# A two-layer encoder trunk on one core: VectorE's transposes in groups of four between weight splits, also in the first step; norm weights in four pieces; rope angles later; the last gate ahead of the next stage's units

## The chip, the cores and the metric

The kernel runs on one core of a Trainium2 chip. The time is device microseconds (us) of one execution. The kernel before took 1093.1 us (median of 3 runs, 1093.0 to 1094.49). All matrix products run on TensorE (PE in the profile), element-wise work on VectorE (DVE), ScalarE (ACT) and GpSimd (POOL); SyncE (SP) only issues DMAs.

## The reference

Two layers (`l`), each of four sublayers, and each sublayer followed by a LayerNorm of the residual. Sequence 256, width 1024, hidden width 2816. Cut to what matters:

```python
def reference(x, mem, positions, ln_g, ln_b, ...):
    for l in range(DEPTH):
        x = layer_norm(ALPHA * x + 0.5 * swiglu(x, ffn1_w13[l], ffn1_w2[l]), ln_g[l, 0], ln_b[l, 0])
        h = x @ w_in[l]
        ...
        y_pool = pool_mixer(u_pool, pool_w[l], pool_scale[l])
        y_mla = mla_mixer(c_q, c_kv, k_pe, positions, q_norm_g[l], w_uq[l], kv_norm_g[l], w_ukv[l])
        y_mix = jnp.concatenate([y_pool, y_mla], axis=-1) @ w_out[l]
        x = layer_norm(ALPHA * x + y_mix, ln_g[l, 1], ln_b[l, 1])
        x = layer_norm(ALPHA * x + memory_cross_attention(x, mem, ...), ln_g[l, 2], ln_b[l, 2])
        x = layer_norm(ALPHA * x + 0.5 * swiglu(x, ffn2_w13[l], ffn2_w2[l]), ln_g[l, 3], ln_b[l, 3])

def swiglu(x, w13, w2):
    gate, up = jnp.split(x @ w13, 2, axis=-1)
    return (jax.nn.silu(gate) * up) @ w2

def layer_norm(x, g, b):                  # in f32
    y = (x - mean(x)) * rsqrt(var(x) + LN_EPS) * g + b
```

Everything is f32.

## The kernel before

**Products and units.** Each f32 matrix is used as a rounded part (hi) and a remainder (lo), both in the type f32r, and a product is three matmuls: hi·hi, hi·lo, lo·hi. Weights come in 366 units of 128x1024 numbers. SP loads a unit into one of four `raw` slots, ScalarE rounds it (`split_hi`, L1180), VectorE subtracts (`split_lo`, L1429), and TensorE takes it from one of six slots (`w_hi`/`w_lo`, and two cut from `v_flat` and `cqp`). SP waits for `lo_done` of the unit four before: a raw slot comes free when VectorE is through with it.

**Order.** Each engine's program is written out by hand in the same order of stages: `ffn(0,0)`, norm 0, `mix(0)` (projection, pool mixer, attention, `w_out`), norm 1, `memory(0)`, norm 2, `ffn(0,1)`, norm 3, and the same for layer 1. Norms are numbered `e` = 0 to 7. TensorE counts milestones on one semaphore, `pe_done`; a `Plan` numbers them before the program is written, and `done[tag]` is the count at which `tag` is reached. `ahead(tag)` on ScalarE and VectorE splits as many of the coming units as find a free slot by that milestone, `ahead_to(n)` all up to unit n.

**A feed-forward stage** has 11 steps (`FS`). With `u` its first unit, a step `s` is four units of w13 (`up`, PSUM banks of 128x512), ScalarE's silu (`gate`, L1222), VectorE's product (`multiply`, L1472) into `ev`, then the 256 tokens x 256 hidden columns are turned into columns, rounded (`round_hidden`, L1230) and split (`split_hidden`, L1492), and two units of w2 follow (`down`). TensorE runs `up(s+1)` before `down(s)`. For steps 1 to 9 (`by_blocks`) VectorE turns the hidden block itself, with 16 STREAM_TRANSPOSEs (L1486) right behind `multiply`; for step 0 and step 10 TensorE does it with four transposes through the identity (`turn_hidden`, L854). Steps 2 to 9 stand in a hardware loop.

**A residual stage** such as `w_out` has eight row units. `row_tail` runs the last five for token block 0 first (milestone `("y", e, 0)`), then `second_block` does token block 1: first its left half for all five (`("half y", e)`), then its right half, and only in that last pass is a unit's milestone counted:

```python
for c in range(2):
    for i, n in enumerate(units):
        ...
        last = row_block(n, acts[i], 1, False, i == len(units) - 1, [c])
        if c == 1:
            reach(last, ("unit", n), *([("y", e, 1)] if i == len(units) - 1 else []))
    if c == 0:
        reach(last, ("half y", e))
```

**A norm** (VectorE's `norm`, odd part for e = 1 and 5): `residual(0, ·)` (L1535), `mean(0)`, `center(0)` (L1546: subtract the mean, times `ln_g`), `variance(0)` (L1551), `residual(1, 0)`, `shift(0)` (L1559: times the reciprocal deviation that GpSimd made at L1815, plus `ln_b`), then one unit split, `residual(1, 1)` and the same for token block 1. TensorE transposes the normed block (`turn`, L674) as soon as `norm_done` says so, block 0 right behind the row stage and block 1 inside the next filler product. `gb` holds `ln_g` and `ln_b`, each spread over all 128 partitions; GpSimd loads it (`load_gains`, L1808, two DMAs of 512 KB), for norms 1 and 5 after the pool mixer, which uses `gb` as scratch, for norm 0 after the rope tables, whose angles are made in `gb` too, and else when the norm before is finished. `center` waits for all of a norm's DMAs:

```python
dve.wait_ge(gains_landed, 32 * (e + 1))
```

## Time and profile before

| | before |
|---|---|
| median of 3 runs | 1093.1 us (1093.0 to 1094.49) |
| the profiled execution | 1093.56 us |
| its span | 1091.7 us |
| PE busy | 1081.4 us, 5720 matmuls |
| DVE busy | 847.9 us, 1450 instructions |
| ACT busy | 534.4 us, 731 instructions |
| POOL busy | 80.8 us, 120 instructions |
| read from memory | 201.41 MB, 185 GB/s over the span |

Busy is the time in which an engine had an instruction in work; the span is the time from the first to the last instruction. The execution is 1.9 us longer than its span. In the rows further down, a timeline row is start, duration, engine, line, operation, what it writes and reads, its shapes, and how many instructions it merges; in square brackets the idle time before it and what ended it. Matmuls overlap in their ends: a row's duration holds the way through the array, so one matmul of 512 columns shows 0.39 us while the next one starts 0.23 us after it.

### The profile page before, as it was taken

How to read it: one execution, taken by the hardware profiler on the slowest of the kernel's cores; microseconds unless marked ns; L12 is line 12 of the kernel's file. 1: busy time of each engine (PE TensorE's matmuls, PEld its weight loads, DVE VectorE, ACT ScalarE, POOL GpSimd, SP SyncE). 2: the span in 40 equal slices, each digit the busy share in tenths (PEclk: the TensorE clock that was granted, in tenths of full speed). 3: DMA queues.
4: the chain of work that ended last, by engine and by line, in shares of the span. 5: the costliest groups of instructions: out<-in, count | busy, mean ns of one | idle time of the engine just before them, and what ended most of it. 6: DMA issues, size and time to landing. Idle time of an engine off the chain costs nothing.

```text
span 1091.7 us, 16584 instructions
## 1 busy us (share of the span) xinstructions
PE 1081.4 (99%) x5720; PEld 934.6 (86%) x5720; DVE 847.9 (78%) x1450; ACT 534.4 (49%) x731; POOL 80.8 (7%) x120
## 2 busy tenths in 40 slices
PE   9999999999999999999999999999999999999997
PEld 8788888999999888888888888889999988888885
DVE  5888877797765778778687887878977777887885
ACT  5545444556464554444454444445664646444442
POOL 0260000140100100000010000001401000000000
PEclk9999999999999999999999999999999999999999
DMA  8666766354664475665666557554446555556551
GB/s 301 194 210 193 230 194 220 112 166 163 198 207 149 154 231 177 214 188 179 210 191 222 173 184 226 169 194 124 162 155 205 182 171 193 177 189 214 174 188 58
DMA packets 156803, 203.18 MB, mean 186 GB/s; under 512 B 12656, under 2 KB 137840, under 8 KB 156752
## 3 DMA queue, kind: packets, MB, share of 16 engines
...
HBM read 201.41 MB, written 1.05 MB: 185 GB/s over the span
## 4 chain that ended last, share of the span: by engine, by line
PE 96%; DVE 2%; issue 1%; DMA 0%; ACT 0%; POOLq 0%; DVEq 0%; SPq 0%; POOL 0%
PE ps L591 93%; PE ps L674 1%; DVE w_lo L1429 1%; DVE hidden_T L1486 0%; PE ps L1118 0%; DMA raw<-in_ffn_w 0%; PE ps L854 0%; DVE memT L1462 0%; DVE mixT L1492 0%; PE ps L942 0%; PE ps L1088 0%; PE ps L995 0%; PE ps L1047 0%; DVE x L1535 0%; PE ps L1049 0%
## 5 line engine op out<-in xcount | busy, mean ns | idle before, releaser
L1180 ACT CAST w_hi<-raw 128x1024 fp32r<-128x1024 f32 (+1 forms) x247 | 255.8, 1044 | 213.2 <-PE ps L591 97.3
L1429 DVE TENSOR_TENSOR w_lo<-raw,w_hi 128x1024 fp32r<-128x1024 f32 (+1 forms) x247 | 295.7, 1222 | 77.7 <-ACT w_hi L1180 75.9
L591 PE MATMUL ps<-w_hi,xT 128*128 128x512 f32 (+1 forms) x912 | 287.1, 389 | 0.0
L591 PEld LDWEIGHTS ps<-w_hi,xT 128*128 128x128 f32 x912 | 171.0, 188 | 35.1 <-issue 0.4
L591 PE MATMUL ps<-w_hi,mixT 128*128 128x512 f32 x688 | 198.1, 390 | 0.5 <-DVE mixT L1492 0.5
L1180 ACT CAST v_flat<-raw 128x1024 fp32r<-128x1024 f32 (+1 forms) x114 | 118.5, 1045 | 138.5 <-DMA raw<-in_ffn_w 70.0
L1486 DVE STREAM_TRANSPOSE hidden_T<-ev 32x128 f32<-32x128 f32 x576 | 174.4, 303 | 8.6
L591 PE MATMUL ps<-v_flat,xT 128*128 128x512 f32 (+1 forms) x660 | 177.2, 389 | 0.0
L591 PE MATMUL ps<-w_lo,xT 128*128 128x512 f32 (+1 forms) x456 | 175.3, 388 | 0.0
L591 PEld LDWEIGHTS ps<-w_hi,mixT 128*128 128x128 f32 x688 | 128.7, 188 | 27.3 <-DVE v_flat L1429 1.0
L591 PEld LDWEIGHTS ps<-v_flat,xT 128*128 128x128 f32 x660 | 123.7, 188 | 25.4 <-DVE cqp L1429 0.2
L591 PE MATMUL ps<-w_lo,mixT 128*128 128x512 f32 x344 | 109.9, 389 | 0.0
L591 PEld LDWEIGHTS ps<-w_lo,xT 128*128 128x128 f32 x456 | 85.6, 188 | 17.2 <-DVE w_lo L1422 0.4
L1429 DVE TENSOR_TENSOR v_flat<-raw,v_flat 128x1024 fp32r<-128x1024 f32 (+3 forms) x59 | 71.8, 1217 | 28.2 <-ACT v_flat L1180 27.9
L591 PE MATMUL ps<-v_flat,mixT 128*128 128x512 f32 x340 | 89.4, 390 | 0.1
L1429 DVE TENSOR_TENSOR cqp<-raw,v_flat 128x1024 fp32r<-128x1024 f32 (+1 forms) x55 | 67.2, 1221 | 27.1 <-ACT v_flat L1180 26.7
L591 PEld LDWEIGHTS ps<-w_lo,mixT 128*128 128x128 f32 x344 | 64.6, 188 | 13.4
L591 PEld LDWEIGHTS ps<-v_flat,mixT 128*128 128x128 f32 x340 | 63.7, 188 | 13.6 <-DVE mixT L1492 0.5
L1815 POOL TENSOR_TENSOR st<-st,cst 128x1 f32<-128x1 f32 x16 | 15.3, 956 | 796.2 <-DVE st L1551 796.2
L591 PE MATMUL ps<-cqp,xT 128*128 128x512 f32 (+1 forms) x132 | 51.2, 388 | 0.0
L591 PE MATMUL ps<-w_hi,memT 128*128 128x256 f32 x256 | 48.3, 285 | 0.0
L1472 DVE TENSOR_TENSOR ev<-ps,ev 128x512 f32<-128x512 f32 x44 | 30.3, 690 | 22.3 <-ACT ev L1222 22.1
...
## 6 DMA issues: line engine op xcount, KB each, us to landing
...
raw<-in_ffn_w SPq DMA_DIRECT2D x88, 512.0 KB, 5.1
raw<-in_mem_wkv SPq DMA_DIRECT2D x32, 512.0 KB, 4.8
raw<-in_w_out SPq DMA_DIRECT2D x16, 512.0 KB, 4.1
raw<-in_mem_wq SPq DMA_DIRECT2D x16, 512.0 KB, 5.6
raw<-in_mem_wo SPq DMA_DIRECT2D x16, 512.0 KB, 4.7
gb<-in_ln_g POOLq DMA_DIRECT2D x8, 512.0 KB, 4.3
gb<-in_ln_b POOLq DMA_DIRECT2D x8, 512.0 KB, 6.1
```

Of the source, the lines that this page charges most:

```text
L591: return nc.tensor.matmul(dst, stand, move, start=start, stop=stop, skip_group_check=True)
L674: last = nc.tensor.transpose(ps[:, 4 + 2 * b + c, (k % 4) * P:(k % 4 + 1) * P], src[:, k * P:(k + 1) * P], ident)
L1180: nc.scalar.copy(slot_hi[slot[n]][:, 0:size], raw[:, n % RAW, 0:size]).then_inc(hi_done, 1)
L1429: nc.vector.tensor_tensor(slot_lo[slot[n]][:, s], raw[:, n % RAW, s], slot_hi[slot[n]][:, s].bitcast(F32), ALU.subtract).then_inc(lo_done, 1)
L1472: last = nc.vector.tensor_tensor(h, step_banks(m + 2 * s)[:, :, S:2 * S], h, ALU.mult)
L1486: last = nc.vector.transpose(hT[j:j + BLOCK, :, :, i:i + BLOCK], h[i:i + BLOCK, :, :, j:j + BLOCK])
L1815: nc.gpsimd.tensor_tensor(RSTD[b], VEPS[b], cst[:, C_HALF:C_HALF + 1], ALU.pow)\
```

## The change

1. **First step by blocks.** For `e` = 3, 4 and 7, VectorE also turns the hidden block of step 0, and TensorE's four transposes there go (`by_blocks(e, s)`; stage `e` = 0 keeps them).
2. **Groups of four.** The 16 STREAM_TRANSPOSEs no longer stand behind `multiply`; they come in four groups of four, each ahead of one weight split, and in step 0 in pairs of groups ahead of the splits up to `u + 8` and `u + 9`.
3. **Norm weights in four pieces.** `ln_g` and `ln_b` come in halves of 256 KB; each piece is issued when a unit of the stage under way is done on TensorE, and `center` waits for all four.
4. **Angles later.** The positions and rope angles start after unit 23 instead of unit 11, in `pw` in place of `gb`; `pool_w` goes into `pw` after the tables, and norm 0's weights no longer wait for the tables.
5. **Gate first.** At a stage's end ScalarE and VectorE split only up to the stage's last unit (`u + 6 * FS`) before `gate(10)` and `multiply(10)`, where `ahead` also took a unit of the next stage.

```diff
-    BLOCK_TURNED = FS - 2
+    BLOCK_TURNED = FS - 1
...
-        def by_blocks(s):
+        def by_blocks(e, s):

-            return 0 < s < FS - 1
+            return e + s > 0 and s < FS - 1
...
-                        if j == 1 and s == 1:
+                        if j == 1 and s == 1 and e == 0:
                             turn_hidden(0)
...
                 gate(0)
-                ahead_to(u + 7) if e == 0 else ahead(("hidden", e, 0))
+                ahead_to(u + (7 if e == 0 else 9))
                 round_hidden(0)
...
-                ahead(("item", m + 2 * FS - 1))
+                ahead_to(u + 6 * FS)
                 gate(FS - 1)
...
-                def turn_blocks(s, it):
+                def turn_blocks(s, i, it=None):
...
-                    for i in range(0, P, BLOCK):
-                        for j in range(0, P, BLOCK):
-                            last = nc.vector.transpose(hT[j:j + BLOCK, :, :, i:i + BLOCK], h[i:i + BLOCK, :, :, j:j + BLOCK])
-                    last.then_inc(hidden_turned, 1)
+                    tokens = slice(i * BLOCK, (i + 1) * BLOCK)
+                    for j in range(0, P, BLOCK):
+                        last = nc.vector.transpose(hT[j:j + BLOCK, :, :, tokens], h[tokens, :, :, j:j + BLOCK])
+                    if i == P // BLOCK - 1:
+                        last.then_inc(hidden_turned, 1)
...
                 multiply(0)
-                ahead_to(u + 7) if e == 0 else ahead(("hidden", e, 0))
+                if e == 0:
+                    ahead_to(u + 7)
+                else:
+                    for i in range(P // BLOCK):
+                        turn_blocks(0, i)
+                        if i % 2:
+                            ahead_to(u + 8 + i // 2)
                 split_hidden(0)
...
-                        for n in range(first + 6 * s, first + 6 * s + 4):
-                            split_lo(n, it)
+                        for i in range(4):
+                            turn_blocks(s + 1, i, it)
+                            split_lo(first + 6 * s + i, it)
                         split_hidden(s + 1, it)
...
                 def center(b):
                     dve.wait_ge(mean_ready, 2 * e + b + 1)
-                    dve.wait_ge(gains_landed, 32 * (e + 1))
+                    dve.wait_ge(gains_landed, 64 * (e + 1))
...
             def load_gains(e):
+                l, k = e // 4, e % 4
+                first, apart = {0: (plan["ffn", l, 0]["units"] + (41 if e == 0 else 5), 3), 1: (plan["wout", l]["units"], 1),
+                                2: (plan["wq", l]["units"], 2), 3: (plan["ffn", l, 1]["units"] + 5, 3)}[k]
                 for i, w in enumerate(("ln_g", "ln_b")):
-                    pool.dma_start(gb[:, i, :], a[w][e // 4, e % 4:e % 4 + 1, :].partition_broadcast(P))\
-                        .then_inc(gains_landed, 16)
+                    for c in range(HALVES):
+                        cols = slice(c * D // 2, (c + 1) * D // 2)
+                        pool.wait_ge(pe_done, done["unit", first + apart * (2 * i + c)])
+                        pool.dma_start(gb[:, i, cols], a[w][l, k:k + 1, cols].partition_broadcast(P))\
+                            .then_inc(gains_landed, 16)
...
-            pool.wait_ge(pe_done, done["unit", plan["ffn", 0, 0]["units"] + 11])
+            pool.wait_ge(pe_done, done["unit", plan["ffn", 0, 0]["units"] + 23])
...
-            pool.wait_ge(tables_done, 1)
             load_gains(0)
+            pool.wait_ge(tables_done, 1)
+            own(nc.gpsimd.memset(pw[:, :, :, :], 0.0))
+            for l in range(L):
+                for g in range(len(POOL_WINDOWS)):
...
```

On GpSimd, between the pool mixer of layer 0 (it ends with `gb<-poolM,gb`) and the reciprocal deviations of norm 1 (`st<-st,cst`), before:

```order
L1862 TENSOR_TENSOR gb<-poolM,gb 128x512 [waits pool_step]
L1808 DMA gb<-in_ln_g 128x1024 [waits pool_split]
L1808 DMA gb<-in_ln_b 128x1024
L1815 TENSOR_TENSOR st<-st,cst 128x1 [waits var_ready] x2
L1808 DMA gb<-in_ln_g 128x1024 [waits norm_done]
```

and now:

```order
L1881 TENSOR_TENSOR gb<-poolM,gb 128x512 [waits pool_step]
L1826 DMA gb<-in_ln_g 128x512 [waits pe_done,pool_split]
L1826 DMA gb<-in_ln_g 128x512 [waits pe_done]
L1826 DMA gb<-in_ln_b 128x512 [waits pe_done] x2
L1833 TENSOR_TENSOR st<-st,cst 128x1 [waits var_ready] x2
```

Two DMAs that waited for the pool mixer alone are four that each wait for a milestone of TensorE. With `first` the first unit of `w_out` and `apart` 1, these are the milestones of its units 0, 1, 2 and 3; units 0 to 2 are whole row units, unit 3 is the first of `row_tail`'s five. The plan of the changed kernel numbers them 128, 129, 131 and 134 for norm 1, with `("y", 1, 0)` at 132, `("half y", 1)` at 133 and `("y", 1, 1)` at 138; for norm 5 they are 376, 377, 379 and 382, with 380, 381 and 386.

On VectorE, in the first step of the stage `e` = 3, from the product of step 0 (`ev<-ps,ev`) to the product of step 1, before:

```order
L1472 TENSOR_TENSOR ev<-ps,ev 128x512 [waits silu_done]
L1429 TENSOR_TENSOR w_lo<-raw,w_hi 128x1024 [waits hi_done]
L1429 TENSOR_TENSOR v_flat<-raw,v_flat 128x1024 [waits hi_done]
L1429 TENSOR_TENSOR cqp<-raw,v_flat 128x1024 [waits hi_done]
L1429 TENSOR_TENSOR w_lo<-raw,w_hi 128x1024 [waits hi_done]
L1492 TENSOR_TENSOR mixT<-ps,mixT 128x2x2x128 [waits columns_hi]
L1429 TENSOR_TENSOR w_lo<-raw,w_hi 128x1024 [waits hi_done] x2
L1472 TENSOR_TENSOR ev<-ps,ev 128x512 [waits silu_done]
L1486 STREAM_TRANSPOSE hidden_T<-ev 32x2x2x32 [waits bank_free]
L1486 STREAM_TRANSPOSE hidden_T<-ev 32x2x2x32 x15
```

and now:

```order
L1473 TENSOR_TENSOR ev<-ps,ev 128x512 [waits silu_done]
L1487 STREAM_TRANSPOSE hidden_T<-ev 32x2x2x32 [waits bank_free]
L1487 STREAM_TRANSPOSE hidden_T<-ev 32x2x2x32 x7
L1430 TENSOR_TENSOR w_lo<-raw,w_hi 128x1024 [waits hi_done]
L1487 STREAM_TRANSPOSE hidden_T<-ev 32x2x2x32 x8
L1430 TENSOR_TENSOR v_flat<-raw,v_flat 128x1024 [waits hi_done]
L1494 TENSOR_TENSOR mixT<-hidden_T,mixT 128x2x2x128 [waits columns_hi]
L1430 TENSOR_TENSOR cqp<-raw,v_flat 128x1024 [waits hi_done]
L1430 TENSOR_TENSOR w_lo<-raw,w_hi 128x1024 [waits hi_done] x3
L1473 TENSOR_TENSOR ev<-ps,ev 128x512 [waits silu_done]
```

Sixteen STREAM_TRANSPOSEs stand ahead of the hidden split, and the four unit splits that stood there are two; the rest come behind it. In the loop, VectorE's row now is, from the product of a step:

```order
L1473 TENSOR_TENSOR ev<-ps,ev 128x512 [waits silu_done]
L1484 REGISTER_ALU
L1487 STREAM_TRANSPOSE hidden_T<-ev 32x2x2x32 [waits bank_free]
L1487 STREAM_TRANSPOSE hidden_T<-ev 32x2x2x32 x3
L1428 REGISTER_ALU
L1430 TENSOR_TENSOR w_lo<-raw,w_hi 128x1024 [waits hi_done]
L1487 STREAM_TRANSPOSE hidden_T<-ev 32x2x2x32 x4
L1428 REGISTER_ALU
L1430 TENSOR_TENSOR w_lo<-raw,w_hi 128x1024 [waits hi_done]
```

where before all sixteen stood behind the product and the splits followed. The number of instructions up to the hidden split is the same.

## Rows read from the trace of the kernel before

**Rows 1.** the page: busy time of the engines, and the chain by engine

```profile
PE 1081.4 (99%) x5720; PEld 934.6 (86%) x5720; DVE 847.9 (78%) x1450; ACT 534.4 (49%) x731; POOL 80.8 (7%) x120
...
PE 96%; DVE 2%; issue 1%; DMA 0%; ACT 0%; POOLq 0%; DVEq 0%; SPq 0%; POOL 0%
```

**Rows 2.** what TensorE waited for: us in total, times, longest

```profile
PE ps L591 <- DVE w_lo L1429: 0.8, 1, 0.8
PE ps L591 <- DVE mixT L1492: 0.5, 1, 0.5
```

**Rows 3.** timeline of all engines, norm 1, token block 0

```profile
280.68 1.28 DVE L1546 SCALAR_TENSOR_TENSOR tmp<-x,st,gb 128x1024 f32<-128x1024 f32 x1
...
282.48 0.69 DVE L1535 SCALAR_TENSOR_TENSOR x<-ps,x 128x512 f32<-128x512 f32 x1 [0.38 <-PE ps L591]
...
282.74 0.39 PE L591 MATMUL ps<-w_hi,mixT 128*128 128x512 f32 x1
...
283.22 1.42 DVE L1559 SCALAR_TENSOR_TENSOR x<-tmp,st,gb 128x512 f32<-128x512 f32 x2
...
285.69 1.04 PE L674 MATMUL ps<-cst,x 128*128 128x128 f32 x8
285.89 0.69 DVE L1535 SCALAR_TENSOR_TENSOR x<-ps,x 128x512 f32<-128x512 f32 x1 [1.26 <-PE ps L591]
```

**Rows 4.** timeline of TensorE, norm 1, token block 1

```profile
290.88 1.28 PE L674 MATMUL ps<-cst,x 128*128 128x128 f32 x8
```

**Rows 5.** timeline of TensorE round the four transposes of step 0, stage e = 3

```profile
386.73 0.39 PE L591 MATMUL ps<-w_hi,xT 128*128 128x512 f32 x1
386.96 0.60 PE L854 MATMUL ps<-cst,ev 128*128 128x128 f32 x4
387.31 0.48 PE L591 MATMUL ps<-w_hi,xT 128*128 128x512 f32 x1
```

**Rows 6.** timeline of all engines, step 1 of the first stage

```profile
37.80 0.69 DVE L1472 TENSOR_TENSOR ev<-ps,ev 128x512 f32<-128x512 f32 x1
...
38.52 5.05 DVE L1486 STREAM_TRANSPOSE hidden_T<-ev 32x128 f32<-32x128 f32 x16
...
48.97 0.72 PE L591 MATMUL ps<-w_hi,mixT 128*128 128x512 f32 x2 [0.54 <-DVE mixT L1492]
```

**Rows 7.** timeline of all engines, steps 0 and 1 of stage e = 3

```profile
382.35 0.69 DVE L1472 TENSOR_TENSOR ev<-ps,ev 128x512 f32<-128x512 f32 x1 [0.87 <-ACT ev L1222]
...
384.92 1.23 DVE L1429 TENSOR_TENSOR v_flat<-raw,v_flat 128x1024 fp32r<-128x1024 f32 x1 [0.30 <-ACT v_flat L1180]
...
390.96 1.05 ACT L1180 CAST w_hi<-raw 128x1024 fp32r<-128x1024 f32 x1 [1.22 <-DMA raw<-in_ffn_w]
...
393.79 0.69 DVE L1472 TENSOR_TENSOR ev<-ps,ev 128x512 f32<-128x512 f32 x1 [0.53 <-ACT ev L1222]
```

**Rows 8.** what GpSimd waited for: us in total, times, longest

```profile
POOL gb L1808 <- ACT sinR L1261: 90.8, 1, 90.8
```

**Rows 9.** DMA issues: what, queue, count, KB each, median us to landing

```profile
gb<-in_ln_g POOLq DMA_DIRECT2D x8, 512.0 KB, 4.3
...
gb<-in_positions POOLq DMA_DIRECT2D x2, 0.5 KB, 2.3
```

**Rows 10.** the line L1808 (GpSimd's loads of norm weights), issue to landing

```profile
DMA to landing us min/median/max: 3.8/5.4/7.4
```

**Rows 11.** busy us by engine in a stretch, then PEclk, DMA share, GB/s

```profile
284.00:286.00 2.00, 2.00 (x12) 1.64 (x11) 0.74 (x2) 0.27 (x1) 0.00 (x0) 1.00 0.03 8
```

**Rows 12.** timeline of all engines, norm 5, token block 0

```profile
824.18 1.28 DVE L1546 SCALAR_TENSOR_TENSOR tmp<-x,st,gb 128x1024 f32<-128x1024 f32 x1
...
829.39 0.69 DVE L1535 SCALAR_TENSOR_TENSOR x<-ps,x 128x512 f32<-128x512 f32 x1 [1.26 <-PE ps L591]
```

**Rows 13.** timeline of TensorE at the start of the program

```profile
1.06 2.93 PE L1118 MATMUL ps<-ev 128*128 128x128 f32 x12 [1.06 <-DVE ev L1776]
...
4.00 1.97 PE L674 MATMUL ps<-cst,x 128*128 128x128 f32 x8
```

More of the change, by code:

```diff
@@ L212, in plan_ffn @@
         for s in range(1, FS):
-            marks += [UNIT_] * 2 + ([[("hidden", e, 0)]] if s == 1 else []) + (turned(2) + turned(3) if e == 0 and s == 1 else [])
+            marks += [UNIT_] * 2 + ([[("hidden", e, 0)]] if e == 0 and s == 1 else []) + (turned(2) + turned(3) if e == 0 and s == 1 else [])
             marks += [UNIT_, ["U", "I", "I"]] + [UNIT_] * (2 * (s < FS - 1))
@@ L478, in trunk @@
         poolB = tiles(gb[:, 1, 0:512], 2)
+        pw_flat = pw[:, :, :, :].rearrange("p l t c -> p (l t c)")
         def by_head(t):
@@ L726, in ffn @@
             def ffn(l, w):
-                e, f, turns = 4 * l + 3 * w, (2 * l + w) * FS, 2 * (2 * l + w)
+                e, f = 4 * l + 3 * w, (2 * l + w) * FS
                 blocks = (2 * l + w) * BLOCK_TURNED
@@ L862, in wait_hidden @@
                 def wait_hidden(s, it=None):
-                    if by_blocks(s):
+                    if by_blocks(e, s):
                         pe.wait_ge(hidden_lo, plus(blocks + s, it, STEPS))
@@ L1225, in round_hidden @@
                 def round_hidden(s, it=None):
-                    if by_blocks(s):
+                    if by_blocks(e, s):
                         act.wait_ge(hidden_turned, plus(blocks + s, it, STEPS))
@@ L1520, in ffn @@
                 state["next"] = first + LOOP_UNITS * LOOPS
-                ahead(("unit", plan["ffn", l, w]["units"] + 6 * (FS - 1) - 2 + 1))
+                for i in range(P // BLOCK):
+                    turn_blocks(FS - 2, i)
+                    ahead_to(first + LOOP_UNITS * LOOPS + min(i + 1, 3))
+                ahead(("unit", u + 6 * (FS - 1) - 2 + 1))
                 split_hidden(FS - 2)
-                ahead(("item", m + 2 * FS - 1))
+                ahead_to(u + 6 * FS)
                 multiply(FS - 1)
@@ L1826, in rope_angles @@
                 n = TB * HALF
-                ang, turns, part_of = gb[:, 0, 2 * n:3 * n], gb[:, 0, 3 * n:4 * n], gb[:, 0, 4 * n:5 * n]
-                own(nc.gpsimd.tensor_copy(gb[:, 1, TB:2 * TB], gb[:, 1, 0:TB].bitcast(I32)))
+                ang, turns, part_of = (pw_flat[:, k * n:(k + 1) * n] for k in (2, 3, 4))
+                places = pw_flat[:, 5 * n:5 * n + 2 * TB]
+                own(nc.gpsimd.tensor_copy(places[:, TB:2 * TB], places[:, 0:TB].bitcast(I32)))
                 for b in range(TB):
                     own(nc.gpsimd.tensor_scalar(ang[:, b * HALF:(b + 1) * HALF], cst[:, C_FREQ:C_FREQ + HALF],
-                                                gb[:, 1, TB + b:TB + b + 1], None, ALU.mult))
+                                                places[:, TB + b:TB + b + 1], None, ALU.mult))
                 for i, quarter in enumerate((0.25, 0.0)):
-                    r = gb[:, 0, i * n:(i + 1) * n]
+                    r = pw_flat[:, i * n:(i + 1) * n]
                     own(nc.gpsimd.tensor_scalar(turns, ang, 1.0 / (2.0 * math.pi), quarter, ALU.mult, ALU.add))
@@ L1862, in pool_group @@
                 nc.gpsimd.tensor_tensor(poolB, poolM[:, :, :], poolU, ALU.subtract).then_inc(pooled, 1)
-            own(nc.gpsimd.memset(pw[:, :, :, :], 0.0))
             clear_keys()
-            pool.wait_ge(pe_done, done["unit", plan["ffn", 0, 0]["units"] + 11])
+            pool.wait_ge(pe_done, done["unit", plan["ffn", 0, 0]["units"] + 23])
             for b in range(TB):
-                pool.dma_start(gb[:, 1, b:b + 1].bitcast(I32),
+                place = 5 * TB * HALF + b
+                pool.dma_start(pw_flat[:, place:place + 1].bitcast(I32),
                                a["positions"][0, b * P:(b + 1) * P].rearrange("(p o) -> p o", o=1)).then_inc(pos_landed, 16)
@@ L1871, in _ @@
             for l in range(L):
-                for g in range(len(POOL_WINDOWS)):
-                    rows = slice((g % 2) * 64, (g % 2 + 1) * 64)
-                    pool.dma_start(pw[rows, l, g // 2, rows], a["pool_w"][l, g]).then_inc(small_landed, 16)
                 for t in range(2):
@@ L1879, in _ @@
                     pool.dma_start(dst, a[w][l:l + 1, :].partition_broadcast(P)).then_inc(small_landed, 16)
+            load_gains(0)
             pool.wait_ge(tables_done, 1)
-            load_gains(0)
+            own(nc.gpsimd.memset(pw[:, :, :, :], 0.0))
+            for l in range(L):
+                for g in range(len(POOL_WINDOWS)):
+                    rows = slice((g % 2) * 64, (g % 2 + 1) * 64)
+                    pool.dma_start(pw[rows, l, g // 2, rows], a["pool_w"][l, g]).then_inc(small_landed, 16)
             for l in range(L):
```

20 lines of the change are left out of this document (10 added, 10 removed).

## The prediction

> **What bounds the kernel now.** I read the page's busy times and its chain first. TensorE is busy 1081.4 of 1091.7 us, and 96% of the chain that ended last is TensorE [rows 1]. So no other engine's work counts by itself: a change gains what it takes off TensorE's list or out of TensorE's waits, and costs what it puts in. The waits come second. TensorE's waits are a handful; the two largest are 0.8 and 0.5 us [rows 2]. Removing every wait would be worth some 3 us.
>
> The places that matter are therefore those where TensorE today waits for nothing but has little room. The timeline of the norm behind `w_out` is the third view. There VectorE starts `center(0)` at 280.68, `shift(0)` at 283.22, and TensorE takes the normed block at 285.69 without a pause [rows 3]. Block 1 follows inside the filler product, where eight transposes take 1.28 us [rows 4] against 1.04 for the same eight at 285.69 [rows 3]: the 0.24 us between is a wait for the second `shift`. Room at the first: 285.69 - (283.22 + 0.71) = 1.8 us. At the second: none. Whatever delays VectorE in this norm arrives on TensorE almost whole.
>
> **The change part by part.**
>
> *First step by blocks (1).* TensorE loses 3 x 4 transposes. Before them a 512-column matmul starts at 386.73, and the next would start 0.23 us on, at 386.96; it starts at 387.31, 0.35 later, and it holds 0.09 longer than the usual 0.39 (0.48) [rows 5]. So 0.44 us for a stage, 1.3 us for three. In exchange VectorE has 16 more transposes (5.05 us, as in [rows 6]) in each, between the product and the hidden split of step 0. For stage e = 3: the product starts at 382.35 [rows 7] and ends at 383.04; two groups of four (2.5), a unit split (1.2), two groups (2.5), a unit split (1.2), hidden split (0.7) give 391.1. TensorE wants it after `up(1)`; without the transposes that stage's third unit starts at 386.96, and a unit is 12 matmuls at 0.227 us, 2.72: 386.96 + 2 x 2.72 = 392.4. It is in time by 1.3 us. What suffers is the next link. The split of unit u + 8 is now at 389.3 to 390.5 instead of 384.92; it frees the raw slot for unit u + 12, whose rounding came 4.8 us after the old one's end (386.15 to 390.96) [rows 7]. Now that is 395.3, and the product of step 1, which stands behind it, goes from 393.79 to about 397.6. From the product's start to the end of the hidden split VectorE needs 0.7 + 5.05 + 4 splits (4.7) + 0.7 = 11.2 us, so 408.8; TensorE wants it after two units of `down(0)` and four of `up(2)`: 392.4 + 6 x 2.72 = 408.7. A few tenths may be lost, at most 0.5; for e = 7 the same sum comes out even, for e = 4 with 0.8 us to spare.
>
> *Groups of four (2).* In the loop VectorE's order has the same instructions up to the hidden split, so it ends at the same place. In the first stage the step 1 split is already late: product at 37.80, transposes from 38.52, and TensorE starts at 48.97, 11.2 later, after 0.54 us idle [rows 6]. That wait stays. Changing between transposes and splits costs the overlap of neighbours, about 0.1 a time, so it may grow by 0.2. The raw slots come free more evenly, up to 3.7 us sooner, but no wait of TensorE in the loop is put down to a weight that came late; worth nothing. Parts 1 and 2 together: -1.3 + 0.2 + 0.4 = -0.7 us, between -1.4 (no new wait) and +1.
>
> *Angles later (4) and gate first (5).* Neither touches an instruction that TensorE waits for in the trace of before. GpSimd was through with angles and small loads 90.8 us before ScalarE's tables let it go on [rows 8]; a start two steps of the loop later (2 x 16.4 us) leaves 58 of them. What cover there is for the clearing of `pw` and its eight loads is the rest of the stage and norm 0. Zero. The gate part is hidden by the row tail, in which TensorE needs none of the next stage's units; if that cover failed it would cost a split, 1.2 us.
>
> *Norm weights in four pieces (3).* This adds a wait, and here the sum is made. For the six norms other than 1 and 5 the four milestones are units ahead of the stage's row tail, all passed long before the norm begins: no cost. For norms 1 and 5 the fourth piece waits for milestone 134 (382), and the plan has ("y", e, 0) at 132 and ("half y", e) at 133. `center(0)` follows 132 and waits for all four pieces. So it can't start before a piece that is issued after "half y".
> - "half y" lets VectorE's residual(1, 0) start at 282.48; the three matmuls of unit 3's right half end with the one at 282.74, at 283.13 [rows 3]. GpSimd issues at about 283.2.
> - How long a 256 KB piece takes to land the trace does not show. A load of 0.5 KB from GpSimd took 2.3 us, the 512 KB loads 4.3 in the median of `ln_g` [rows 9], 3.8 at the least, 5.4 in the median of both and 7.4 at most [rows 10]. From 284 to 286 us the DMA engines moved 8 GB/s, 3% of their time [rows 11]: the piece has them for itself, so the lower rows are near. Bounds 2.3 and 5.4; I take the middle between 2.3 and the undisturbed 4.2 or so, 3.2 us. It lands at 286.4.
> - `center(0)` starts at 286.45 in place of 280.68. From its start to the end of `shift(0)` the trace has 283.22 + 1.42 - 280.68 = 3.96 us, so 290.4. Queued behind on VectorE: residual(1, 1), a unit split, block 1's norm. residual(1, 1) started at 285.89 [rows 3]; now 290.4. That is 4.5 us, and since block 1 has no room on TensorE, TensorE loses 4.5 us: about 4.0 ahead of block 0's transposes, the rest ahead of the second half of block 0 and of block 1.
> - Norm 5 has the same intervals: center 824.18, residual(1, 1) 829.39, 5.21 us apart, as in norm 1 (280.68, 285.89) [rows 12]. Again 4.5.
>
> Together 9.0 us; with the landing at 2.3 it would be 7.2, at 5.4 13.4.
>
> The Trainium skill ("DMA: Bandwidth & Descriptors", section "Anatomy of one DMA — SWDGE (gpsimd) path") states a fixed part of about 2.0 us plus the bytes at 436 GB/s. By that rule a piece takes an estimated 2.6 us, and norms 1 and 5 together would cost 7.8 us. The trace sides with the fixed part (2.3 for almost no bytes [rows 9]) and is slower on the rest (3.8 at least for 512 KB [rows 10], where the rule has 3.2). It is the rule that speaks against cutting a load in pieces that come late: the fixed part does not get smaller.
>
> Sum: -1.3 + 0.6 + 9.0 = +8.3 us. The profiled execution took 1093.56, so 1101.9; the median of the runs is 0.46 lower, and I predict 1101.4 us.
>
> **The rivals.**
>
> *A. TensorE's clock falls in the pause.* The program starts on the lower of the two clock levels (1.2 GHz): eight transposes at 4.00 take 1.97 us [rows 13], the same eight 1.04 at 285.69 [rows 3]. What came before was no work at all. If a pause of 4 us is enough for that, work at half rate follows; at the start that went from 1.06 to 5.97 at the least [rows 13], 4.9 us, in which 2.5 us are lost. One fall: 1103.9; both: 1106.4. Against it: nothing in the trace pauses longer than 1 us in mid program, so it shows neither. The Trainium skill ("TensorE: Matmul & The Clock Gate", Part 1) says that TensorE left idle goes back to half rate, and that this bites in the middle of kernels; no pause in this trace is long enough to test it. I give one fall or two 25%, because the pause is several times longer than any that the trace shows without one.
>
> *B. The fourth piece is not late.* If the wait's milestone is met sooner than I read (a unit counted at its first use, say), or the landing is hidden, only parts 1 and 2 remain: 1093.1 - 0.7 = 1092.4, not slower. The price sets in where `center(0)` starts later than 281.9, since residual(1, 1) had 1.26 us of waiting for TensorE ahead of it [rows 3]. For it: the other six norms work so. Against: the quoted loop counts the unit only at c = 1. 7%.
>
> *C. The hidden split of step 0 becomes the late one.* 16 transposes in the first step, three stages, each 1 us later than by the sum above: 3 us more, 1104.4. Against: 1.3 us in hand by the sum above. 8%.
>
> **How the numbers follow.** My forecast, late fourth pieces alone: 60%; A 25%, B 7%, C 8%. The forecast's own range is 1099.5 (landing 2.3) to 1105.8 (5.4). The range for 8 in 10 reaches into A and C and leaves B out: 1098.5 to 1107. A difference within 0.2% (2.2 us) is what a measurement of this kernel can't tell from none. Faster by more than that would need B and all small waits gone: 2%. Within: 6%. Slower: 92%.
>
> **What would show it.** In the changed kernel's profile the waits of TensorE must have a new largest group, the transposes of normed rows (L674 before) behind VectorE's `x`, two waits of about 4 us, near 285 and 827 us. VectorE must stand idle some 5.8 us ahead of `center(0)` of norms 1 and 5, released by a DMA of `gb`; the other six norms must show nothing. The timeline must have one DMA of GpSimd right behind "half y" there. Matmuls drop from 5720 to 5708, the transposes of hidden blocks from 32 to 20. Step 1 of the first stage keeps its wait of 0.5 to 1 us. The slices' PEclk tells A: a digit under 9 behind either pause. If TensorE has no pause at 285, my reading of the milestones is wrong and the whole plus goes. If the pauses are there and the total is not, the rest was given back where TensorE waits today.

## The result and the profile after

| | before | changed |
|---|---|---|
| median | 1093.24 us (1093.0 to 1094.49, 4 runs) | 1106.62 us (1106.25 to 1107.13, 4 runs) |
| ratio to before | | 1.0119, 95% interval 1.0103 to 1.0135 |
| the profiled execution / its span | 1093.56 / 1091.7 us | 1107.13 / 1105.3 us |

The change makes the kernel 13.4 us slower. The forecast was 1101.4 us; rival A, both pauses followed by a lower clock, had 1106.4. The changed kernel's page, its busy times, the granted clock in 40 slices of the span and the chain by engine [rows 1]:

```profile
PE 1085.0 (98%) x5708; PEld 937.6 (85%) x5708; DVE 866.4 (78%) x1498; ACT 534.2 (48%) x731; POOL 88.4 (8%) x136
...
PEclk9999999999899999999999999999998999999999
...
PE 91%; DVE 4%; DMA 2%; issue 2%; ACT 1%; SPq 0%; POOL 0%; POOLq 0%; DVEq 0%; ACTq 0%
```

Matmuls are 12 fewer, as the change says. Of the chain, 5 points went from TensorE to VectorE, DMA, issue and ScalarE. Two slices of the clock, the eleventh and the thirty-first, show an 8; they hold 276 to 304 and 829 to 857 us. What TensorE waited for, in total, times, longest [rows 2]:

```profile
PE ps L675 <- DVE x L1571: 8.4, 2, 4.2
PE ps L592 <- DVE mixT L1494: 1.3, 2, 0.8
```

The first row is new: twice 4.2 us for the normed block (`turn` is L675 now, `shift` L1571). The timeline of norm 1, all engines, shows where it comes from [rows 3] (`load_gains` is L1826, `center` L1558, `residual` L1547):

```profile
283.88 0.54 POOL L1826 DMA_DIRECT2D gb<-in_ln_b  x1 [10.34 <-PE ps L592]
...
287.60 1.28 DVE L1558 SCALAR_TENSOR_TENSOR tmp<-x,st,gb 128x1024 f32<-128x1024 f32 x1 [6.50 <-DMA gb<-in_ln_b]
...
289.73 1.41 DVE L1571 SCALAR_TENSOR_TENSOR x<-tmp,st,gb 128x512 f32<-128x512 f32 x2 [0.17 <-POOL st L1833]
...
290.53 1.97 PE L675 MATMUL ps<-cst,x 128*128 128x128 f32 x8 [4.23 <-DVE x L1571]
291.06 0.68 DVE L1547 SCALAR_TENSOR_TENSOR x<-ps,x 128x512 f32<-128x512 f32 x1
```

GpSimd issues the fourth piece at 283.88, VectorE stands 6.50 us until it lands, and TensorE stands 4.23 us. Then the eight transposes take 1.97 us in place of 1.04 [rows 3]. Norm 5 is a copy [rows 12]:

```profile
837.80 1.28 DVE L1558 SCALAR_TENSOR_TENSOR tmp<-x,st,gb 128x1024 f32<-128x1024 f32 x1 [6.48 <-DMA gb<-in_ln_b]
...
840.72 1.97 PE L675 MATMUL ps<-cst,x 128*128 128x128 f32 x8 [4.20 <-DVE x L1571]
```

Busy time by engine, granted clock, DMA share and GB/s in short stretches behind the first pause and round the second [rows 11]:

```profile
285.00:290.00 5.00, 1.30 (x6) 0.75 (x4) 2.23 (x5) 0.00 (x0) 0.57 (x1) 0.92 0.23 52
...
288.00:289.00 1.00, 0.00 (x0) 0.00 (x0) 1.00 (x3) 0.00 (x0) 0.00 (x0) 1.00 0.00 0
289.00:290.00 1.00, 0.00 (x0) 0.00 (x0) 0.83 (x3) 0.00 (x0) 0.57 (x1) 0.61 0.00 0
...
290.00:292.00 2.00, 1.47 (x7) 1.47 (x8) 1.96 (x6) 0.00 (x0) 0.00 (x0) 0.50 0.00 0
...
294.00:296.00 2.00, 2.00 (x11) 2.00 (x11) 2.00 (x4) 2.00 (x3) 1.09 (x1) 0.50 0.84 247
296.00:300.00 4.00, 4.00 (x36) 4.00 (x36) 2.24 (x3) 1.20 (x3) 0.00 (x0) 0.99 0.24 82
...
839.00:842.00 3.00, 1.28 (x6) 1.28 (x7) 2.80 (x9) 0.00 (x0) 0.57 (x1) 0.50 0.01 3
842.00:845.00 3.00, 3.00 (x16) 3.00 (x15) 2.82 (x5) 2.78 (x5) 1.27 (x1) 0.50 0.11 29
```

The seventh figure is the clock. It is 1.00 until 289, falls between 289 and 290 while TensorE does nothing, and is 0.50 (1.2 of 2.4 GHz) from 290 to 296, with 11 matmuls in 2 us, where the same two microseconds of a kernel at full rate hold 19 (further down, in "The clock, once more"). The 52 GB/s over 285 to 290 are 260 KB, the piece and nothing else. The Trainium skill ("TensorE: Matmul & The Clock Gate", Part 1) says that a TensorE left idle goes back to half rate in the middle of a kernel; this trace agrees, in both norms (pauses of 4.23 and 4.20 us, then 0.50).

Where the 13 us arose can be read by laying the two traces over each other: for each matmul, its start in the changed kernel less the start of the same matmul before. That lag grows in these places (us):

| place | norm 1 | stage e = 3 | e = 4 | norm 5 | e = 7 | first stage |
|---|---|---|---|---|---|---|
| the pause | +4.38 | | | +4.36 | | |
| behind it, to 299 and 849 us | +2.28 | | | +2.00 | | |
| four transposes gone | | -0.49 | -0.47 | | -0.48 | |
| hidden split late | | +0.89 | | | | +0.22 |

With +0.3 in the program's first 10 us, for which I have no cause (the other traces have -0.25 to +0.38 there), this is 13.0 us; the last matmul is 13.18 late. The two memory stages add 0.14 each, which the table leaves out. (Behind the pauses the lag first grows by 2.55 and 2.26, up to where the clock is back, and then falls by 0.26, the waits for block 1 that the kernel before had.) The other two late places, stage e = 3 and the first stage, in the timeline of TensorE [rows 6]:

```profile
416.74 1.64 PE L592 MATMUL ps<-v_flat,mixT 128*128 128x512 f32 x6 [0.59 <-DVE mixT L1494]
...
49.47 0.72 PE L592 MATMUL ps<-w_hi,mixT 128*128 128x512 f32 x2 [0.76 <-DVE mixT L1494]
```

### The profile page after: what moved, and what is told of

Its sections match the earlier page's. It is cut to its first block, busy times and chain, and to the rows that moved or that the text cites. A ratio compares the mean times of both kernels' runs of the same rounds, so it can differ in the third digit from the quotient of the medians.

```text
span 1105.3 us, 16631 instructions
## 1 busy us (share of the span) xinstructions
PE 1085.0 (98%) x5708; PEld 937.6 (85%) x5708; DVE 866.4 (78%) x1498; ACT 534.2 (48%) x731; POOL 88.4 (8%) x136
## 4 chain that ended last, share of the span: by engine, by line
PE 91%; DVE 4%; DMA 2%; issue 2%; ACT 1%; SPq 0%; POOL 0%; POOLq 0%; DVEq 0%; ACTq 0%
PE ps L592 89%; PE ps L675 1%; DMA raw<-in_ffn_w 1%; DVE hidden_T L1487 1%; DVE w_lo L1430 1%; DMA gb<-in_ln_b 1%; DVE tmp L1558 0%; SPq L541 0%; DVE mixT L1494 0%; DVE memT L1463 0%; DVE x L1571 0%; PE ps L855 0%; ACT w_hi L1181 0%; DVE v_flat L1430 0%; PE ps L943 0%
## 5 line engine op out<-in xcount | busy, mean ns | idle before, releaser
L1430 DVE TENSOR_TENSOR w_lo<-raw,w_hi 128x1024 fp32r<-128x1024 f32 (+1 forms) x247 | 299.3, 1222 | 52.9 <-ACT w_hi L1181 50.4
L1487 DVE STREAM_TRANSPOSE hidden_T<-ev 32x128 f32<-32x128 f32 x624 | 189.0, 303 | 11.2
L592 PEld LDWEIGHTS ps<-w_lo,mixT 128*128 128x128 f32 x344 | 64.6, 188 | 13.4
L1223 ACT ACTIVATE ev<-ps 128x512 f32<-128x512 f32 x44 | 26.3, 597 | 69.3 <-PE ps L592 69.3
L1231 ACT CAST mixT<-hidden_T 128x512 fp32r<-128x512 f32 x39 | 24.3, 622 | 63.8 <-DVE hidden_T L1487 63.8
```

What stands on the lines that cost most here:

```text
L592: return nc.tensor.matmul(dst, stand, move, start=start, stop=stop, skip_group_check=True)
L1223: nc.scalar.activation(ev[:, (f + s) % 2, :].rearrange("p (b c) -> p b c", b=TB), step_banks(m + 2 * s)[:, :, 0:S], ACT.Silu).then_inc(sil ...
L1231: nc.scalar.copy(hidden_columns(s, 0), hidden_source(e, s, m)).then_inc(columns_hi, 1)
L1430: nc.vector.tensor_tensor(slot_lo[slot[n]][:, s], raw[:, n % RAW, s], slot_hi[slot[n]][:, s].bitcast(F32), ALU.subtract).then_inc(lo_done, 1)
L1487: last = nc.vector.transpose(hT[j:j + BLOCK, :, :, tokens], h[tokens, :, :, j:j + BLOCK])
```

## The experiments

All are edits of the changed kernel unless said otherwise. "Lag" is against the kernel before, as above.

**Fourth piece early.** Norms 1 and 5 issue their fourth piece at the third's milestone, ahead of `("y", e, 0)`.

```diff
-    pool.wait_ge(pe_done, done["unit", first + apart * (2 * i + c)])
+    pool.wait_ge(pe_done, done["unit", first + min(apart * (2 * i + c), 2 if k == 1 else 9)])
```

> The changed kernel with the fourth piece of norm 1's and norm 5's weights issued at the same milestone as the third (unit 2 of w_out), all else as changed. Theory (the late fourth piece is the whole of the loss): TensorE's two waits of 4.2 us ahead of the transposes of normed rows and the half-rate stretches behind them go, 2 x 6.6 us, so about 1093.3 us, within 1 us of the kernel before. Rival (part of the loss is the cutting itself, or VectorE's new order): 1096 us or more.

1094.75 us (1093.83 to 1099.1; two of the twelve runs are above 1098, the rest below 1095), ratio 1.0019 (1.0009 to 1.0028). The norm has its old times: `center` starts at 280.67 and no DMA is waited for, and both waits of `turn` are gone.

```profile
280.67 1.28 DVE L1558 SCALAR_TENSOR_TENSOR tmp<-x,st,gb 128x1024 f32<-128x1024 f32 x1
282.19 0.57 POOL L1833 TENSOR_TENSOR st<-st,cst 128x1 f32<-128x1 f32 x1 [8.59 <-DVE st L1563]
```

So 11.9 of the 13.4 us hang on one milestone. What is left is +1.5 us where my sum had -0.7 for parts 1 and 2. No term of mine explains that; the later runs look for it. Its lag steps are -0.36 and +0.92 in stage e = 3, -0.47 and -0.48 in the others, and +0.49 and +0.73 in the memory stages (near 319 and 863 us).

**Pieces alone.** The kernel before with part 3 alone.

```diff
+    for c in range(HALVES):
+        pool.wait_ge(pe_done, done["unit", first + apart * (2 * i + c)])
+        pool.dma_start(gb[:, i, cols], ...)
...
-    dve.wait_ge(gains_landed, 32 * (e + 1))
+    dve.wait_ge(gains_landed, 64 * (e + 1))
```

> The kernel before with part 3 alone (four pieces at the changed kernel's milestones; for norm 0 still behind the tables). Theory (part 3 is the whole loss, parts 1, 2, 4 and 5 together come to about nothing): 1106.5 us. Rival (the other parts share in it): 1103 us or less.

1106.64 us, ratio 1.0132 (1.0117 to 1.0146): the whole loss. TensorE's waits, and two windows behind the pause:

```profile
PE ps L674 <- DVE x L1559: 8.4, 2, 4.3
```

```profile
290.00:292.00 2.00, 2.00 (x11) 1.90 (x10) 1.97 (x5) 1.06 (x2) 0.00 (x0) 0.50 0.03 8
292.00:294.00 2.00, 2.00 (x15) 2.00 (x14) 1.82 (x4) 2.00 (x6) 1.54 (x1) 0.72 0.38 121
```

The clock falls here too, but is back sooner (0.72 in 292 to 294, where the changed kernel had 0.50). The pauses are +4.33 and +4.42, and the lag grows by 1.63 and 1.71 more while the clock is down (2.55 and 2.26 in the changed kernel, read the same way).

**Only `shift` waits.** The two pieces of `ln_b` get a semaphore of their own, for which `shift` waits; `center` waits for `ln_g` alone.

```diff
-    dve.wait_ge(gains_landed, 64 * (e + 1))      # in center
+    dve.wait_ge(gains_landed, 32 * (e + 1))
...
+    dve.wait_ge(biases_landed, 32 * (e + 1))     # in shift
```

> The changed kernel with ln_b's pieces on a semaphore of their own, for which shift waits and not center. The fourth piece stays as late, but less work stands behind it: TensorE's pause is 2.2 us instead of 4.4. Theory (a pause this short leaves the clock alone): 2.2 to 2.5 us lost a norm, about 1098.2 us with PEclk full throughout. Rival (any pause of this kind takes the clock down): 4.8 us more, about 1103 us.

1101.46 us, ratio 1.0069 (1.0055 to 1.0084), about half the loss. The timeline of norm 1:

```profile
281.02 1.28 DVE L1559 SCALAR_TENSOR_TENSOR tmp<-x,st,gb 128x1024 f32<-128x1024 f32 x1
...
287.42 1.41 DVE L1573 SCALAR_TENSOR_TENSOR x<-tmp,st,gb 128x512 f32<-128x512 f32 x2 [3.90 <-DMA gb<-in_ln_b]
288.22 1.32 PE L676 MATMUL ps<-cst,x 128*128 128x128 f32 x8 [2.04 <-DVE x L1573]
```

`center` goes at its old time, the pause is 2.04 us, and the transposes run at full rate behind it. In norm 5, with a pause of 2.09, the clock did fall: the lag there goes up 2.24 in the pause and 1.6 behind it, against 2.19 and 0.35 in norm 1. So near 2 us it goes either way, in one execution. The trace is of the slowest of the four runs; its mean granted clock is 0.996, and that of the fastest, 1099.58 us, is 0.998, as in the traces without a fall. That run is the nearest to the theory's 1098.2.

**The pause filled.** To take the clock alone, 37, then 19 idle matmuls of 128 columns stand ahead of the first `turn` of norms 1 and 5 (the 37 come out of a reading that one takes 0.11 us).

```diff
+    if e % 4 == 1:
+        take_bank(busy_bank)
+        for _ in range(37):      # 19 in the second
+            nc.tensor.matmul(bank(busy_bank)[:, 0:P], ident, ident, start=True, stop=True)
     first()
```

> The changed kernel, with 37 idle matmuls of 128 columns (about 4 us at the full clock) on TensorE ahead of the transposes of norms 1 and 5, written to a bank that the next product overwrites. The piece stays late. Theory (the pause costs 4.4 us a time and the half-rate clock behind it 2.4 more): the clock stays full, about 1101.8 us. Rival (the slow stretch behind the pause is VectorE's late chain, and the clock costs nothing beside it): about 1106.5 us, unchanged.

1112.6 us, ratio 1.0173 (1.0158 to 1.0188). A miss of mine in the sizing: each idle matmul is two in the trace, 74 in all, and they took 8.42 us, twice the pause. The clock did stay up, behind both. With 19:

> As the run with 37 idle matmuls of the changed kernel, with 19: each is issued as two passes of 0.11 us (74 records took 8.4 us there), so 19 fill 4.2 us, the length of the pause. Theory (the half-rate clock costs 2.4 us behind each pause): the clock stays full, 4.8 us under the changed kernel, about 1101.8 us. Rival (the clock is free beside VectorE's late chain): 1106.5 us.

1108.12 us (1106.28 to 1113.51), ratio 1.013 (1.0114 to 1.0146), no gain. The trace is of the slowest run, 1113.51. In it the lag behind norm 1 grew by 0.3 in place of 2.3. But the memory stage behind that lost 4.1, and the stage e = 4 another 4.0, where the changed kernel loses 0.14 and nothing. In both places TensorE waited over 2 us, and the clock fell there. Its waits, and the clock behind the first of them and behind the second (a pause of 2.27 us before 610.08):

```profile
PE ps L592 <- DVE mixT L1500: 4.5, 3, 2.3
PE ps L592 <- DVE qT L1447: 3.1, 2, 2.4
```

```profile
326.00:328.00 2.00, 1.40 (x6) 1.40 (x7) 0.55 (x1) 0.00 (x0) 0.00 (x0) 0.63 0.38 115
328.00:330.00 2.00, 2.00 (x12) 2.00 (x11) 1.39 (x2) 0.25 (x1) 0.00 (x0) 0.52 0.49 201
610.00:612.00 2.00, 1.92 (x5) 1.54 (x6) 2.00 (x2) 2.00 (x3) 0.00 (x0) 0.50 0.79 270
```

Each of the two cost about 2.5 in the pause and 1.6 at half rate. The page's slices show 9 in all 40 places here: a fall this short does not take a slice of 28 us under nine tenths. In the memory stage norm 2's four pieces are issued between weight loads; hence the next run.

**Norm 2's pieces at once.** With the early fourth piece, norms 2 and 6 issue all four pieces when the norm before is finished.

```diff
+    if k != 2:
         pool.wait_ge(pe_done, done["unit", ...])
```

> The kernel with the early fourth piece (1094.75 us), and the four pieces of norms 2 and 6 issued as soon as the norm before is finished, not one by one through the wq stage. Theory (a piece beside mem_wq's loads makes VectorE late for the first scores): TensorE's waits for qT (0.7 us in two) and the two steps behind it (0.5 and 0.7 us by matmul starts) go, so about 1093.6 us. Rival (these steps come from elsewhere): 1094.7 us, unchanged.

1093.98 us, ratio 1.0004 (0.9995 to 1.0013): 0.8 less than with the early piece alone, where 1.1 was expected, and no wait for `qT` is left. The two kernels' intervals overlap, so the steps in the traces carry this more than the medians do. The timelines of GpSimd, first with the milestones, then at once:

```profile
297.02 0.58 POOL L1826 DMA_DIRECT2D gb<-in_ln_g  x1 [7.10 <-PE ps L592]
302.52 0.54 POOL L1826 DMA_DIRECT2D gb<-in_ln_g  x1 [4.92 <-PE ps L592]
308.28 0.54 POOL L1826 DMA_DIRECT2D gb<-in_ln_b  x1 [5.22 <-PE ps L592]
314.04 0.54 POOL L1826 DMA_DIRECT2D gb<-in_ln_b  x1 [5.22 <-PE ps L592]
```

```profile
292.60 1.12 POOL L1827 DMA_DIRECT2D gb<-in_ln_g  x2 [1.82 <-DVE x L1571]
293.71 1.07 POOL L1827 DMA_DIRECT2D gb<-in_ln_b  x2
```

Spread over 20 us, the pieces cost TensorE the two steps of +0.49 and +0.73; issued in 2 us, nothing. All traces agree: the five kernels that issue them at once have no step in either memory stage, and the eight that wait for the milestones have 0.08 to 4.1 in the first and 0.14 to 1.97 in the second. That it is contention with the weight loads, I infer from the place; no run measured it by itself.

**The clock, once more.** The changed kernel's late fourth piece with norm 2's pieces at once, without and with the 19 idle matmuls.

```diff
+    if k != 2:
         pool.wait_ge(pe_done, done["unit", first + apart * (2 * i + c)])
...
+    for _ in range(19): ...      # the second only
```

> The changed kernel with its late fourth piece in norms 1 and 5; only the four pieces of norms 2 and 6 are issued at once when the norm before is finished, without waits for TensorE's milestones. If these pieces' waits cost what they cost with the early fourth piece (1094.75 to 1093.98, 0.8 us), the time is 1105.8 us with both pauses at half rate behind them; if the changed kernel does not pay for them at all, 1106.6. It is the pair of the next run.

> The same as e9_late_at_once, with 19 idle matmuls of 128 columns ahead of the first transposes in norms 1 and 5, which fill 4.4 us of the pause. If the stretch behind the pause is longer only because TensorE's clock fell (about 2.3 us a norm, less 0.3 us by which the idle matmuls end later than the pause), the time falls by 4.0 us against e9_late_at_once: 1101.8 if that one is at 1105.8, and the turn's eight transposes take 1.04 to 1.3 us in place of 1.97. If VectorE, late since the pause, sets the pace behind it, the clock gives nothing: within 1 us of e9_late_at_once.

1105.84 us, ratio 1.0115 (1.01 to 1.0131), and 1107.8 us, ratio 1.0138 (1.0123 to 1.0154). The first is what was expected. The second missed the 1101.8 by 6. TensorE's timeline in norm 1, first without, then with idle matmuls, and the clock behind them:

```profile
290.18 1.97 PE L675 MATMUL ps<-cst,x 128*128 128x128 f32 x8 [4.25 <-DVE x L1571]
```

```profile
285.88 4.40 PE L727 MATMUL ps<-cst 128*128 128x128 f32 x38
290.42 1.32 PE L675 MATMUL ps<-cst,x 128*128 128x128 f32 x8
```

```profile
294.00:296.00 2.00, 2.00 (x19) 1.96 (x18) 2.00 (x4) 2.00 (x3) 0.98 (x1) 1.00 0.85 262
```

Locally the theory holds: the filled pause starts the transposes 0.24 later, and the kernel gains 1.9 us on its pair over norm 1 (its lag on the pair goes from +0.10 ahead of the pause to -1.77 at 298.5) and 2.0 over norm 5 (+0.37 to -1.67). That is the clock's price where it arises, and against the kernel before at most 0.3 is left behind the pause for VectorE's lateness. (The trace without idle matmuls is of a run at a mean clock of 0.992; two of its four runs, at 0.995, took 1104.74 and 1104.93, so their half-rate stretches were shorter and cheaper.) But the gain is not kept. In the profiled run, itself the fastest of the four at 1105.1, stage e = 3 takes back 0.47 and stage e = 4 1.64. In the latter TensorE waits for the hidden split, and ScalarE and VectorE have waited for the weights (timelines of e = 4, first TensorE, then ScalarE and VectorE):

```profile
604.46 0.72 PE L592 MATMUL ps<-w_hi,mixT 128*128 128x512 f32 x2 [1.36 <-DVE mixT L1500]
```

```profile
596.34 1.05 ACT L1187 CAST w_hi<-raw 128x1024 fp32r<-128x1024 f32 x1 [2.87 <-DMA raw<-in_ffn_w]
...
597.42 1.23 DVE L1436 TENSOR_TENSOR w_lo<-raw,w_hi 128x1024 fp32r<-128x1024 f32 x1 [1.41 <-ACT w_hi L1187]
```

A weight that lands late holds VectorE's split, and since part 2 of the change puts the transposes behind splits, it holds the hidden block as well. Before, all sixteen stood ahead of the splits. In part TensorE also came too early: on the pair this hidden split ends at 603.75, here at 604.32, 0.57 later, while TensorE is 1.27 sooner, so more than half of the wait is gained time that the loads and VectorE could not follow. The other three runs, 1107.45 to 1108.61, have no trace, but their mean granted clock is on record: 0.997, 0.996 and 0.996, where the profiled run has 0.999 and every trace without a fall 0.998 or 0.999. The trace with a single fall ("Only `shift` waits") has 0.996 too. So in two of them the clock most likely fell after all, at a place that nothing shows, as it did in the trace of the changed kernel with 19 idle matmuls. What put them above the pair's 1104.74 to 1107.01 stays open beyond that.

**Gate first in step 1.** With the early fourth piece, `gate(1)` and `multiply(1)` come ahead of the split of unit u + 12, to make the hidden split of step 1 early.

```diff
-    ahead(("item", m + 3))
-    multiply(1)
     first = loop_first(l, w)
+    ahead_to(first - 1)
+    multiply(1)
+    ahead_to(first)
```

> The kernel with the early fourth piece, and in every feed-forward stage gate(1) and multiply(1) ahead of the split of unit u + 12, which waits for a late raw slot. Theory (step 1's hidden split is late because the product stands behind that split): TensorE's waits for mixT go (1.3 us in two; 0.9 and 0.9 by matmul starts in stages e = 0 and 3), about 1093.0 us. Rival (the raw slots themselves are late, so the loop's first splits wait instead): 1094.7 us, and the wait moves to w_lo or v_flat.

1094.11 us, ratio 1.0007 (0.9998 to 1.0016). In stage e = 3 the step falls from +0.92 to +0.49. In the first stage the wait grows to 1.21 us, though the product is 2 us earlier. The timeline there, first VectorE with the early piece alone, then ScalarE and VectorE with the gate first:

```profile
37.20 0.68 DVE L1473 TENSOR_TENSOR ev<-ps,ev 128x512 f32<-128x512 f32 x1
...
39.34 1.23 DVE L1430 TENSOR_TENSOR w_lo<-raw,w_hi 128x1024 fp32r<-128x1024 f32 x1 [0.18 <-ACT w_hi L1181]
```

```profile
35.22 0.69 DVE L1474 TENSOR_TENSOR ev<-ps,ev 128x512 f32<-128x512 f32 x1
...
38.99 1.05 ACT L1181 CAST w_hi<-raw 128x1024 fp32r<-128x1024 f32 x1 [2.64 <-DMA raw<-in_ffn_w]
40.08 1.22 DVE L1431 TENSOR_TENSOR w_lo<-raw,w_hi 128x1024 fp32r<-128x1024 f32 x1 [1.31 <-ACT w_hi L1181]
```

The same mechanism again: the first split of the loop waits for its load (2.64 us on ScalarE, 1.31 on VectorE), with twelve transposes behind it. The time lies between theory (1093.0) and rival (1094.7), as does the mechanism: stage e = 3 gained, the first stage did not. That wait varies from one execution to the next, though: in the trace of "together" below, with the same order, it is 0.3 us or less.

**TensorE turns step 0 again.** The early fourth piece, with part 1 undone.

```diff
-    return e + s > 0 and s < FS - 1
+    return 0 < s < FS - 1
```

> The kernel with the early fourth piece, without part 1: TensorE turns the hidden block of step 0 in all stages again, VectorE in groups of four from step 1. Theory (part 1 saves 3 x 0.46 us of transposes and gives 0.9 back as a wait in stage e = 3): 0.4 to 0.6 us slower than the early fourth piece alone, 1095.2 us; the wait in e = 3 goes. Rival (16 more transposes a stage cost more than they save): 1094.2 us or less.

1096.24 us, ratio 1.0026 (1.0016 to 1.0035), slower than the 1095.2 expected. The wait of stage e = 3 is gone with the -0.36, -0.47 and -0.48; the three stages are even again. By the last matmul's lag that is 1.5 us slower than the early piece, of which the missing gains of 1.3 less the missing +0.92 explain 0.4. The rest is in the memory stages, +0.67 and +1.47 in place of +0.49 and +0.73, whose waits also vary in the other runs.

**Together, and the best of both.** The early piece, norm 2's pieces at once and the gate first; and a mixed one: the early piece, norm 2's at once, part 1 in stages 4 and 7 alone, and the first stage's sixteen transposes ahead of the splits again.

```diff
-    return e + s > 0 and s < FS - 1
+    return (s > 0 or e > 3) and s < FS - 1
...
-    turn_blocks(s + 1, i, it)
+    for r in (range(4) if i == 0 else ()) if e == 0 else (i,):
+        turn_blocks(s + 1, r, it)
     split_lo(first + 6 * s + i, it)
```

> Early fourth piece in norms 1 and 5, norm 2's and 6's pieces at once, and gate and product of step 1 ahead of the split of unit u + 12. The first two gave 1093.98 us; gate first alone took 0.6 us from 1094.75, of which 0.4 was the wait of stage 3. If the two gains add up: 1093.4, no different from before. If gate first only moves the wait to a later raw slot, as it did in the first stage: 1094.0.

> Early fourth piece, norm 2's and 6's pieces at once, and of the first part of the change only stages 4 and 7 (VectorE turns step 0 there; TensorE turns it in stages 0 and 3), with the first stage's sixteen transposes in a row behind the product as before. By the alignments of the traces: 1093.98 less 0.75 (stage 3: +1.11 gone, -0.36 gone) less 0.2 to 0.4 (first stage's wait) is 1093.0 us, at most 0.3 under the kernel before, which a measurement can't tell from none. The rival: stage 3's later wait comes from the loop's groups and stays, 1094.0.

1093.16 us, ratio 1.0001 (0.9992 to 1.001), and 1092.67 us, ratio 0.9997 (0.9988 to 1.0006), beside 1093.03 for the kernel before. The gains add up, and neither kernel can be told from the one before. What the mixed kernel keeps of the change is worth nothing that its measurement can show. In the mixed one stage e = 3 is clean (the split ends at 407.4, TensorE goes on at 408.88) and the last matmul's lag is -1.24 in the profile; its two longest waits are two that the kernel before has too:

```profile
PE ps L1119 <- DVE ev L1791: 1.1, 1, 1.1
PE ps L592 <- DVE w_lo L1430: 0.8, 1, 0.8
```

## Why the prediction was right, and where it was off

**The mechanism was right.** `center(0)` of norms 1 and 5 waited for a piece issued behind "half y", the six other norms show nothing, and one milestone earlier takes 11.9 us off. The pieces alone make the whole loss. Rival B is out by both, and by the two waits of 4.2 us.

**The late piece was mis-sized, and the two errors cancelled.** I had the issue at 283.2; it was 283.88, of which 0.5 is TensorE's lag at that place (0.46) and 0.2 the way from its matmul's end to the issue. The landing I took as 3.2 us; from the issue to `center` it was 3.7 (3.4 at the least over all pieces), nearer to the undisturbed 512 KB load than to the small one. The estimate of 2.6 us worked out from the Trainium skill ("DMA: Bandwidth & Descriptors", "Anatomy of one DMA — SWDGE (gpsimd) path") was lower still. `center` came at 287.60 where I had 286.45. On the other side, the end of `shift` followed its start by 3.54 us where it had been 3.96, 0.4 sooner, and of VectorE's lateness at most 0.3 us arrived behind the transposes, where I had 0.5. The pauses are 4.38 and 4.36 us; with at most 0.3 behind each they make 8.7 to 9.3 for a forecast of 9.0. That the sum is so near is luck.

**The clock is the step that failed.** The forecast left it at full rate and gave a fall 25%. It fell in both pauses, and 1.9 and 2.0 us of the 6.7 and 6.4 are its price by the pair of traces with and without idle matmuls (2.5 in rival A). Rival A's 1106.4 is what came out, with the right mechanism and some luck in the number: A had 5.0 us for the clock where it was 3.9, and small losses that were in no sum filled the gap (0.5 more in stage e = 3, 0.3 each in the first 10 us and in the memory stages). The range of my own forecast ended at 1105.8; the measured time lies in the wider one only because that reaches into A. The argument against it was that no pause in the trace of before was long enough to show a fall; that is absence of evidence, and the start of the program [rows 13], the only idle stretch there, spoke for it. It deserved more than half of the chance. Two limits stand beside that. Filling the pauses did not make the kernel faster in either try, by the medians: in one profile the clock fell in two other waits instead, in the other 2.1 of the 3.9 us came back as waits behind late weights, and two of that kernel's untraced runs have the mean clock of a run with a fall. And at half rate the pieces alone lost 1.6 us in norm 1 where the changed kernel lost 2.55, so the price depends on when the clock comes back.

**Parts 1 and 2.** The transposes gave 1.44 us for the 1.3 expected. The first stage's wait grew by 0.22 (0.2 expected), but that this fits is luck: in the nine traces with the groups of four, the gate-first ones left out, the step there is +0.02 to +0.83, and in the two others with the old order (the pieces alone, the mixed kernel) it is -0.47 and -0.53, so the 0.54 us wait of the trace of before was itself not the rule. Stage e = 3 lost 0.89 where I had 0.4 and at most 0.5. The chain was as I wrote it, only longer: the product of step 1 started at 405.21, and less the 7.3 us by which TensorE entered the stage late this is 397.9 where the sum had 397.6; from there to the end of the hidden split it took 11.4 (11.2), and TensorE started 0.14 after it, which the sum left out. TensorE was free at 415.99 and started at 416.74. For e = 4 and e = 7 nothing was late. Rival C is right in kind for one stage of three. Stage e = 3 on TensorE again, in two kernels (the mixed one and "TensorE turns step 0 again"), took that wait away; the eight with part 1 and no gate first have 0.8 to 1.55 there.

**Parts 4 and 5** show nothing I can put down to them: behind its four pieces GpSimd still waited 14.0 us for ScalarE's tables.

**What I missed:** "all passed long before the norm begins: no cost" held for `center`, but not for the loads themselves. The pieces of norms 2 and 6 in the memory stages cost 1.2 us together in the kernel with the early piece (0.8 in the medians, against pieces at once), and more in others. In the changed kernel, behind the half-rate stretches, they cost 0.14 each in the trace (medians 1106.62 against 1105.84, a difference within the spread of four runs each).

## What to carry to other kernels

When a load is cut in pieces that are gated on milestones, write down next to each milestone the first instruction that waits for the last piece: here milestone 134 gated a load that the instruction behind 132 needed, and one unit's difference was 1.1% of the kernel. A TensorE pause of some 4 us is priced with the half-rate stretch behind it, unless a row says otherwise, and one of 2 us with a chance of it. To fill such a pause with idle matmuls is worth trying only if what comes behind can use the time. And work that the bound engine waits for should not stand behind work that waits for a load: transposes between splits inherit every late weight.

## What the chip showed beyond that

- TensorE's clock fell to the lower level in pauses of 4.2 to 4.3 us, six times of six in the three profiles that have them. Of four pauses of 2.0 to 2.4 us it fell in or right behind three (2.09, 2.27 and 2.40) and not in the one of 2.04; a pause of 1.72 us, with the 37 idle matmuls, left it up. Behind the longer ones it read 0.50 from 290 to 296 us in the changed kernel and was at 0.72 by 292 to 294 in the kernel with the pieces alone.
- Idle f32 matmuls of 128 columns kept it up over the pause that they filled, six times of six. Each stands in the trace as two, 38 in 4.40 us, 0.116 us each.
- A GpSimd load of 256 KB, alone on the DMA engines, took 3.7 us from issue to the instruction that waited for it. Over all 32 pieces of the changed kernel (the row on `load_gains`):

```profile
DMA to landing us min/median/max: 3.4/4.8/7.2
```

Half the bytes save 0.4 us at the least and 0.6 in the median against the 512 KB loads [rows 10].
